# Weights of the RWKV turns split during the first feed-forward layer and kept in HBM; three float32r matmuls a tile in the pairs; separate signals in the triangular inverse

## The reference

```python
for l in range(2):
    x = x + 0.5 * rmsnorm(swiglu(rmsnorm(x, g1), wg, wu, wd), g2)          # d_ff 2816
    proj = rmsnorm(x, gm) @ w_in[l]                                        # columns A | B | C | G
    oa = rwkv7(A)      # 8 heads x 64, matrix state, token shift, vector decay
    ob = rglru(B)      # conv of width 4, gates, scan
    oc = hgrn2(C)      # 4 heads x 128
    m = (sig(G0)*(oa@proj_a) + sig(G1)*(ob@proj_b) + sig(G2)*(oc@proj_c)) @ w_out
    x = x + rmsnorm(m, gp)
    x = x + 0.5 * rmsnorm(swiglu(rmsnorm(x, g3), wg2, wu2, wd2), g4)
```

## Time and profile before

| | |
|---|---|
| median of 3 runs | 2145.59 us (2145.29 to 2145.84) |
| the profiled execution | 2146.02 us, span on the core 2143.9 us |
| TensorE busy, its clock | 2092.4 us (98%), 1.00 (2.4 GHz) |
| DVE, ACT, POOL busy | 1322.6, 817.9, 39.3 us |
| DMA | 252.13 MB, 118 GB/s over the span |

### The profile page before, as it was taken

How to read it: one execution, slowest core, us unless ns; L and a number is a source line. 1 busy time by engine, 2 the same in 40 slices (tenths; PEclk the granted TensorE clock), 3 DMA queues, 4 the chain that set the end, 5 groups by cost and what they waited for, 6 DMA issues and landing times.

```text
span 2143.9 us, 30994 instructions
## 1 busy us (share of the span) xinstructions
PE 2092.4 (98%) x12624; PEld 1844.9 (86%) x12624; DVE 1322.6 (62%) x1987; ACT 817.9 (38%) x932; POOL 39.3 (2%) x74
## 2 busy tenths in 40 slices
PE   7999999999999999999999999999999999999998
PEld 6999997777766699999999999977777667999998
DVE  4564586776556676555376645766765576765644
ACT  5554451112143145554355534412121422455542
POOL 1000000000000000000000000000000000000000
PEclk9999999999999999999999999999999999999999
DMA  5434431111133243444434443211111323434442
GB/s 210 152 143 157 156 118 38 58 51 70 45 110 120 91 158 118 157 148 147 170 138 146 155 157 138 105 40 52 68 51 65 121 90 130 163 113 149 145 156 103
DMA packets 38067, 252.13 MB, mean 118 GB/s; under 512 B 4720, under 2 KB 4912, under 8 KB 9424
## 3 DMA queue, kind: packets, MB, share of 16 engines
q1 hardware_dynamic: 33120, 234.60, 30.7%
q0 software_dynamic: 4848, 16.13, 2.0%
HBM read 242.05 MB, written 8.67 MB: 117 GB/s over the span
## 4 chain that ended last, share of the span: by engine, by line
PE 85%; DVE 8%; ACT 3%; DVEq 2%; issue 1%; DMA 0%; SPq 0%; ACTq 0%
PE dps L600 42%; PE dps L539 15%; PE dps L489 11%; DVE tmp L1252 2%; PE mx L698 2%; PE mx L692 2%; PE mx L700 2%; ACT tmp L922 1%; PE mx L556 1%; PE mx L809 1%; DVEq L1717 1%; PE mx L845 1%; DVE tmp L1468 1%; DVE rs L1310 1%; DVE tmp L1598 1%
## 5 line engine op out<-in xcount | busy, mean ns | idle before, releaser
L539 PE MATMUL dps<-u,raw 128*128 128x320 f32 x1536 | 478.3, 439 | 0.0
L600 PE MATMUL dps<-uh,whi 128*128 128x320 f32 x1408 | 430.0, 305 | 16.2 <-DVE wlo L1249 15.8
L1249 DVE TENSOR_TENSOR wlo<-raw,whi 128x2048 fp32r<-128x2048 f32 x136 | 311.7, 2292 | 214.7 <-ACT whi L922 209.6
L600 PE MATMUL dps<-uh,wlo 128*128 128x320 f32 x1408 | 434.3, 308 | 0.0
L600 PE MATMUL dps<-ul,whi 128*128 128x320 f32 x1408 | 432.9, 307 | 0.0
L922 ACT ACTIVATE whi<-raw 128x2048 fp32r<-128x2048 f32 x138 | 262.9, 1905 | 380.2 <-PE dps L600 370.0
L539 PEld LDWEIGHTS dps<-u,raw 128*128 128x128 f32 x1536 | 269.5, 190 | 89.2 <-issue 13.7
L600 PEld LDWEIGHTS dps<-uh,whi 128*128 128x128 f32 x1408 | 264.8, 188 | 20.9 <-issue 16.9
L600 PEld LDWEIGHTS dps<-uh,wlo 128*128 128x128 f32 x1408 | 264.9, 188 | 0.0
L600 PEld LDWEIGHTS dps<-ul,whi 128*128 128x128 f32 x1408 | 263.9, 187 | 0.6
L600 PE MATMUL dps<-hfh,whi 128*128 128x320 f32 x704 | 220.4, 313 | 0.0
(11 more groups left out here) (302 smaller groups left out, 3022.1 us busy)
## 6 DMA issues: line engine op xcount, KB each, us to landing
raw<-in_wstream SPq DMA_DIRECT2D x220, 1024.0 KB, 4.8
hs<-in_st_hgrn POOLq DMA_DIRECT2D x8, 512.0 KB, 6.2
out_o_hgrn<-hs POOLq DMA_DIRECT2D x8, 512.0 KB, 2.9
sw<-in_smallw POOLq DMA_DIRECT2D x2, 1024.0 KB, 6.8
ss<-in_st_rwkv POOLq DMA_DIRECT2D x8, 256.0 KB, 3.9
out_o_rwkv<-ss POOLq DMA_DIRECT2D x8, 256.0 KB, 2.3
x<-in_xT SPq DMA_DIRECT2D x4, 320.0 KB, 4.5
out_yT<-x SPq DMA_DIRECT2D x4, 320.0 KB, 2.2
```

The source lines that it names most:

```text
L539: m = pe.matmul(dps[:, 2 * s + c, 0:T], w[:, k, c * P:(c + 1) * P], u[:, k, :], start=k == 0, stop=k == KD - 1, skip_group_check=True)
L600: m = pe.matmul(dps[:, 2 * half + c, 0:T], w[:, k, c * P:(c + 1) * P], v[:, k0 + k, :], start=first and k == 0 and i == 0, stop=last and k ...
L1249: return nc.vector.tensor_tensor(out, a, b, op)
```

## The change

- **Presplit.** In each turn of the first feed-forward loop and once behind it, POOL loads one of the 12 weight blocks of the RWKV turns (two halves of 512 KB, into the memory of `u`), ACT makes its float32r high half (into `wha`), DVE its low half in place (`presplit_hi`, `presplit_lo`), and POOL stores both to a new HBM tensor `split_store` (four stores of 512 KB), then loads the next block. The other kinds of block are loaded as before.
- **Turns.** In the pairs SP loads 24 blocks a layer of `split_store` instead of 12 of weights, each with the high and low part of half a block (`parts0`, `parts1`, in the memory of `raw`). A tile is three float32r matmuls (`turn_pieces`). The normed input is split too: high part `nh` in the memory of x (ACT, `high_normed`), low part `nl` in `wha` and `ovr` (DVE, `low_normed`). x is therefore stored to HBM before the pairs and fetched behind them. The first gate block waits for its buffer until the parts of the last turn are used.
- **Inverse.** `pt_done` becomes `tinv_done` and `tinvt_done`, `t_ready` becomes `tinv_ready` and `tinvt_ready`; from level 2 on the product for `tinvt` lies in other banks of PSUM, so that the next level's first product can start before the subtraction that reads it. The step 0 of `prepare` stands behind the first `tinv`, and steps 4 and 5 both in level 5.
- **Places of the tiles.** 48 tiles a pair as before, 21 instead of 26 of them in the inverse; behind the recurrence the parts of 0, 2, 4, 2, 1, 0, 3, 2 tiles become 1, 3, 5, 2, 1, 2, 3, 2. In HGRN2 head 3 five tiles move to the end of the head. `keep_busy` is 11 instead of 15, and in `border` one scaling stands between two halves of the low input.

The diff shows in turn PE's tiles, SP's loads, POOL's presplit and PE's order in the inverse:

```diff
-        dense_part = pieces(l, B_B + 3 * p, Q_B + 3 * p)
+        dense_part = turn_pieces(l, p)
...
+    def turn_pieces(l, p):
+        done = [0]
+        def some(n):
+            for i in range(done[0], done[0] + n):
+                j, part, c, k = i // 16, i // 8 % 2, i // 4 % 2, i // 8 % 2 * 4 + i % 4
+                b, g = B_B + 3 * p + j, 6 * p + i // 8
+                if i % 16 == 0:
+                    pair_wait(l, (Q_B + 3 * p + j) // 2, b % 2)
+                if i % 8 == 0:
+                    pe.wait_ge(turn_loaded[g % 2], (l * (NTURN // 2) + g // 2) * 16 + 16)
+                    if g < 2:
+                        pe.wait_ge(S["nl_ready"], l * 3 + 2 * g + 1)
+                hi, low = (parts[g % 2][:, a:a + 1024].rearrange("p (k n) -> p k n", k=4) for a in (0, 1024))
+                for t, (w, v) in enumerate(((hi, nh[:, k, :]), (hi, nl[k]), (low, nh[:, k, :]))):
+                    m = pe.matmul(dps[:, 2 * (b % 2) + c, 0:T], w[:, k % 4, c * P:(c + 1) * P], v,
+                                  start=k == 0 and t == 0, stop=k == KD - 1 and t == 2, skip_group_check=True)
+                if i % 8 == 7:
+                    m.then_inc(S["turn_done"], 1)
...
                 order = mixer_order()
-                for j in range(B_A, B_G0):
+                for j in range(B_A, B_B):
                     s = j % 2
                     raw_free(l, j)
                     load(l, 0, order[j - B_A] - s, s)
+                    if j == B_A + 3:
+                        sp.wait_ge(S["x_new"], l * 12 + 8)
+                        sp.dma_start(yT, x[:, :, :]).then_inc(S["x_spilled"], 16)
+                sp.wait_ge(S["presplit"], l * NTURN + NTURN)
+                for g in range(NTURN):
+                    if g < 2:
+                        raw_free(l, B_B + g)
+                    else:
+                        wait_turn(sp, l, g - 2)
+                    sp.dma_start(parts[g % 2][:, :].bitcast(F32), split_store[l * NTURN + g, :, :])\
+                        .then_inc(turn_loaded[g % 2], 16)
                 for j in range(B_G0, B_F2 + 2):
-                    raw_free(l, j)
+                    if j < B_G0 + 2:
+                        wait_turn(sp, l, NTURN - 2 + j - B_G0)
+                    else:
+                        raw_free(l, j)
                     load(l, 0, j - j % 2, j % 2)
+                    if j == B_G0 + 1:
+                        sp.wait_ge(S["x_spilled"], l * 16 + 16)
+                        sp.dma_start(x[:, :, :], yT).then_inc(S["x_back"], 16)
...
+                order = mixer_order()[B_B - B_A:]
+                for q in range(len(order) + 1):
+                    for h in range(2):
+                        g = l * NTURN + 2 * (q - 1) + h
+                        if q:
+                            pool.wait_ge(pre_lo[h], l * len(order) + q)
+                            pool.dma_start(split_store[g, :, 0:1024], pre_high[h].bitcast(F32)).then_inc(pre_stored[h], 16)
+                            pool.dma_start(split_store[g, :, 1024:2048], pre_low[h].bitcast(F32)).then_inc(pre_stored[h], 16)
+                    for h in range(2):
+                        if q:
+                            pool.wait_ge(pre_stored[h], (l * len(order) + q) * 32)
+                            pool.sem_inc(S["presplit"], 1)
+                        if q < len(order):
+                            pool.dma_start(pre_raw[h], wstream[l * NBLK + order[q], :, 1024 * h:1024 * h + 1024])\
+                                .then_inc(pre_loaded[h], 16)
...
-                dense_part(6)
+                dense_part(4)
                 for li in range(1, 6):
                     if li > 1:
-                        dense_part((4, 3, 3, 3)[li - 2])
-                    pe.wait_ge(S["ao_ready"], n * 6 + (li + 1))
-                    pe.wait_ge(S["t_ready"], n * 6 + li)
+                        dense_part(1)
                     if li == 4 and more:
                         key_sums(l, p + 1)
+                    pe.wait_ge(S["ao_ready"], n * 6 + (li + 1))
+                    pe.wait_ge(S["tinv_ready"], n * 5 + li)
+                    if li == 2:
+                        pe.wait_ge(S["tinvt_ready"], n * 5 + 1)
...
-                    dense_part(1)
+                    if li == 5 and more:
+                        rk_sum(l, p + 1)
+                    dense_part(2)
                     pe.wait_ge(S["z_ready"], n * 5 + li)
+                    if li > 1:
+                        pe.wait_ge(S["tinvt_ready"], n * 5 + li - 1)
                     for c in range(nt):
-                        pe.matmul(mx23[:, c * P:(c + 1) * P], tinvt[:, c, :], zs[:, c, :], start=True, stop=True)
+                        m = pe.matmul(mx23[:, c * P:(c + 1) * P], tinvt[:, c, :], zs[:, c, :], start=True, stop=True)
+                    if nt:
+                        m.then_inc(S["tinv_done"], 1)
                     for c in range(nch):
-                        m = pe.matmul(mx01[:, c * P:(c + 1) * P], zs[:, c, :], tinvt[:, c, :], start=True, stop=True)
-                    m.then_inc(S["pt_done"], 1)
-                dense_part(2)
+                        m = pe.matmul(product_at(li, c), zs[:, c, :], tinvt[:, c, :], start=True, stop=True)
+                    m.then_inc(S["tinvt_done"], 1)
+                dense_part(3)
```

More of the change, by code:

```diff
@@ L178, in trunk @@
         rs = sb("rs", T)
-        raw = [sb(f"raw{i}", BLK) for i in range(2)]
+        raw, parts = zip(*[shared(f"raw{i}", BLK, views=[(f"parts{i}", (BLK,))]) for i in range(2)])
         sw, whb = shared("sw", 4, 512, views=[("whb", (BLK,))])
@@ L276, in trunk @@
             rooms[f"P{i}"] = wpc[:, 1024 * i:1024 * i + 1024]
+        uflat = u[:, :, :].rearrange("p a t -> p (a t)")
+        pre_raw, pre_low, pre_high = ([v[:, 1024 * h:1024 * h + 1024] for h in range(2)] for v in (uflat, ulo, wha))
+        nl = [wha[:, T * k:T * k + T] for k in range(6)] + [ovr[:, 0, :], ovr[:, 4, :]]
         def full_half(h):
@@ L312, in trunk @@
         w_loaded = [sem("w_loaded0"), sem("w_loaded1")]
+        pre_loaded, pre_hi, pre_lo, pre_stored, turn_loaded = (
+            [sem(f"{n}{h}") for h in range(2)]
+            for n in ("pre_loaded", "pre_hi", "pre_lo", "pre_stored", "turn_loaded"))
         pair_free = [sem("pair_free0"), sem("pair_free1")]
@@ L476, in block_in @@
             def block_in(l, half, s):
-                pe.wait_ge(w_loaded[s], (l * (NBLK // 2) + half) * 16 + 16)
+                pe.wait_ge(w_loaded[s], landed(l, half))
             def pair_wait(l, qhalf, s):
@@ L986, in read_pair, with presplit_hi @@
                 return fn(dst, dps[:, 2 * s:2 * s + n, 0:T], f)
+            def presplit_hi(l, i):
+                for h in range(2):
+                    act.wait_ge(pre_loaded[h], l * (NTURN * 8) + 16 + i * 16)
+                    fn(pre_high[h], pre_raw[h], ACT.Copy).then_inc(pre_hi[h], 1)
             def ffn(l, b, f):
@@ L1003, in ffn @@
                         split_hi(l, 0, KF + j + 2, j % 2, f)
+                    if f == 0 and j == 1:
+                        presplit_hi(l, KF // 2)
                 if f == 0:
@@ L1172, in _, with high_normed @@
                 read_low_rank(0)
+                def high_normed(i):
+                    act.wait_ge((S["u_half"], S["u_full"])[i], l + 1)
+                    act.wait_ge(S["x_spilled"], l * 16 + 16)
+                    fn(nh[:, 4 * i:4 * i + 4, :], u[:, 4 * i:4 * i + 4, :], ACT.Copy).then_inc(S["nh_ready"], 1)
+                high_normed(0)
                 for h in (10, 11):
@@ L1180, in _ @@
                 high(l, 13)
+                high_normed(1)
                 read_low_rank(2)
@@ L1370, in split_lo, with presplit_lo @@
                 tt(wlo[s][:, :], raw[s][:, :], whi[s][:, :].bitcast(F32), ALU.subtract).then_inc(S["lo_ready"], 1)
+            def presplit_lo(l, i):
+                for h in range(2):
+                    dve.wait_ge(pre_hi[h], l * (NTURN // 2) + 1 + i)
+                    tt(pre_low[h], pre_raw[h], pre_high[h].bitcast(F32), ALU.subtract).then_inc(pre_lo[h], 1)
             def ffn(l, b, f):
@@ L1397, in ffn @@
                     split_lo(l, f, 0, KF + j, j % 2)
+                    if f == 0 and j == 3:
+                        presplit_lo(l, KF // 2)
                     if j in (4, 7, 10):
@@ L1804, in _, with low_normed @@
                 read_a(1)
-                normed(0)
+                normed(0).then_inc(S["u_half"], 1)
                 low_half(l, 8)
                 low_half(l, 9)
+                def low_normed(a, b):
+                    dve.wait_ge(S["nh_ready"], l * 2 + 1 + a // 4)
+                    for k in range(a, b):
+                        m = tt(nl[k], u[:, k, :], nh[:, k, :].bitcast(F32), ALU.subtract)
+                    m.then_inc(S["nl_ready"], 1)
+                low_normed(0, 4)
                 read_a(2)
@@ L1829, in _ @@
                 m.then_inc(S["e_ready"], 1)
+                low_normed(4, 6)
                 read_a(5)
@@ L1832, in _ @@
```

(2 more changed lines are left out.)

117 lines of the change are left out of this document (81 added, 36 removed).

## The result

| | before | changed |
|---|---|---|
| median of four runs | 2145.45 us | 2189.57 us |
| all runs | 2145.29 to 2145.84 | 2186.21 to 2200.73 |
| profiled execution, its span | 2146.0, 2143.9 | 2186.2, 2184.4 |
| mean granted clock | 1.00 | 0.986 |

The changed kernel is slower: the ratio is 1.0214, with a 95% interval of 1.0178 to 1.0251. The forecast was 2124.5 us with a range up to 2150. The sign was wrong, and the time lies outside the range.

What follows compares the result with a forecast made beforehand. PE was taken to bound feed-forward layers and pairs, with a DVE chain close behind in the pairs. -30 + 5.5 + 5.8 - 2.2 = -21 us on 2146.0 gave 2125, median 2124.5 us; range 2112 to 2136, wider 2100 to 2150.

Steps and rivals of the forecast that it cites:

- The presplit loop: First feed-forward layer: load, split, store and next load take 14.1 us against 13.8 a turn, +5.5 us over 22 turns.
- A turn over 15 us: Sign in the first feed-forward layer that the forecast is wrong and the presplit's loop sets the pace.
- The loop's upper bound: Presplit loop in the first feed-forward layer: at most 15.7 us a turn, a loss of 42 us in all.
- The loop of the presplit sets the pace: Rival, first feed-forward layer: 5.24 MB at 340 GB/s makes a turn 15.4 us, total 2154; chance 0.22.
- First turn late: Start of the first feed-forward layer: PE waits for block 3, 2.9 us a layer, +5.8 us in all.
- Arithmetic hidden: First feed-forward loop: the presplit's Copies and subtractions on ACT and DVE are covered, with 0.7 us to spare.
- Pairs, 15.0 us a layer: RWKV pairs: cheaper float32r tiles gain 2.8, 4.1, 4.1 and 4.0 us in pairs 0 to 3, -30 us in two layers.
- Gate block: Pair 3: PE waits 2.7 us for the gate block's load, cutting that pair's gain from 6.7 to 4.0 us.
- HGRN2's end: End of HGRN2 head 3: five tiles cover the idle 1.06 us ahead of the projections, -2.2 us.
- Borders: Borders: four fewer fills of 0.44 us change nothing, as PE waits for DVE; bounds 0 and -1.0 at each of five.
- Parts come late: Rival, pairs: SP's doubled loads lose 1 us on every second part, 24 us, total 2148; chance 0.08.
- PE keeps the whole gain: Rival, pairs and presplit: DVE chains give way and the presplit is hidden, total 2105; chance 0.13.

Runs made afterwards that it cites:

- Raw doubled: The change with raw blocks going alternately to two pairs of half buffers, each load issued a turn ahead, same bytes: 2138.1 us, ratio 0.9949.
- the best kernel: On top of late start, pair 3's two gate tiles moved to its end and HGRN2 head 3's five tiles back in front: 2113.4 us, ratio 0.9849.
- the 64 KB transfers: The changed kernel's own loop with every DMA cut to an eighth of its bytes, except each layer's first block: 2137.9 us.
- the second run: The change with all presplit Copies and subtractions, but only the first block of a layer loaded and stored: 2138.2 us.
- the pairs alone: The change without its presplit loop, one block split a layer and its parts standing in for all 24: 2124.1 us, ratio 0.9901.
- late start: Raw doubled, with no presplit in the loop's first turn and two blocks split in the down part: 2134.4 us.

## Why the prediction was wrong

Between the 2125 us forecast for the profiled execution and the 2186 measured lie 61 us. The presplit has 57 of them (68.2 lost; 11.3 forecast, 5.5 for the loop and 5.8 for the first turn), the end of HGRN2 has 4.

- **The presplit loop, "middle 14.1: 0.25 us a turn, +5.5 us": this step failed.** The mechanism was seen: a loop that must close in a turn. One term of its sum was mis-sized. Arithmetic 2.3 and stores with their hand-overs 6.0 us came within what was taken (2.3 and 4.5 to 6.2). The load was taken as 5.8 to 7.2 us, from a load of the kernel before beside one stream load. The load that the chain waits for took 8.9, beside a stream load, the end of the other half's load and its stores. So the loop took 17.3 instead of 14.1 us. The turn follows the loop from 13.8 us on, so the 32.2 us of layer 0 are 3.4 of the first turn and 2.9 for each of the ten after it, up to 3.3 in the mean of the later ones. A turn over 15 us was the prediction's own sign of this rival, and it is there.
- **The range left out its own bound.** The loop's upper bound, 15.7 us a turn and 42 us in all, gives 2124.5 - 5.5 + 42 = 2161, but the range "from the bounds of the loop and the gate" ends at 2136 and the wider one at 2150. The result lies above 2161 too.
- **The clock had no term.** The trace of before shows none: 1.00 throughout the stretches read. Inside the loop it seems to cost nothing of its own: the chain there holds no TensorE, and half clock takes the place of waiting (22.7 + 10.2 us, against 32.2 us lost in layer 0). That is argued from the trace; no run has the loop without half clock. Outside it costs in full: behind the gate block's wait, and in the pairs.
- **The rival was the right mechanism with the wrong price.** "The loop of the presplit sets the pace", chance 0.22, gave 2154 from bytes over 340 GB/s. Its break-even, 1.2 us a turn, is summed rightly; but its price came from bandwidth, and the loop was bound by its chain. Raw doubled shows both: same bytes, 13.9 us a turn. The Trainium skill's limit of some 358 GB/s a core ("DMA: Bandwidth & Descriptors", Specifications), by which the turn would be 14.6 us by estimate, does not bind this core, which runs alone: 368 GB/s with raw doubled and 376 in the best kernel, both over 50 us. The Trainium skill's price of one DMA, 2.0 us and its bytes at 436 GB/s (same page, Anatomy of one DMA), fits the 64 KB transfers (2.15 us by estimate; 2.2 measured for the loads, 2.4 and 2.6 for the stores). For the whole load it gives an estimated 3.2 us, and the one that the chain waits for took 8.9.
- **First turn late, 2.9 us a layer:** 3.4 us in layer 0 (43.45 to 47.01 between two starts, less 0.14), with a stretch of 6.8 us at half clock that begins in the gap; 5.3 in layer 1, with 3.4 us behind it.
- **Arithmetic hidden:** right, by the second run, where loads come in time.
- **Pairs, 15.0 us a layer:** measured 15.2 and 14.1, in part by luck, since the errors of the parts cancel. Pairs 1 and 2 gained 5.1 each (4.7 in pair 1 of layer 1; forecast 4.1), pair 0 4.1 and 4.2 (2.8), pair 3 with what follows it 0.9 and 0.2 (4.0). What was forecast for pairs 1 and 2 is there: the wait at level 1 is 1.57 us where 2 were forecast, 7.56 us pass from variance product to key transposes, and the tiles start 0.145 us apart:

```profile
418.40 0.31 PE L623 MATMUL dps<-nh,parts 128*128 128x320 f32 x1
418.54 0.31 PE L623 MATMUL dps<-ovr,parts 128*128 128x320 f32 x1
418.69 0.31 PE L623 MATMUL dps<-nh,parts 128*128 128x320 f32 x1
...
436.95 1.24 PE L784 MATMUL mx<-ho 128*128 128x128 f32 x9 [1.57 <-DVE ho L1372]
```

- **Gate block, 2.7 us:** 2.9, as in the list of waits; the load of its block lands 5.2 us after its issue at 597.8. What was missed is again the clock (PE busy, clock, DMA share, GB/s), right behind the wait that ended at 603.1:

```profile
603.00:606.00 3.00, 2.87 (x7) 0.50 0.07 25
607.00:610.00 3.00, 3.00 (x20) 1.00 0.00 0
```

- **HGRN2's end, -2.2 us:** +1.6. The five tiles do fill the idle time ahead of the projections, but cost more behind HGRN2 (1.9 us in layer 0) than they free in it (1.3), and a stretch of half clock falls into head 3 in both layers. With them back in place the stretch is gone.
- **Borders 0:** 56.6 and 56.5 us. Right.
- **Parts come late:** no wait on `parts` in the profile of the change or of the pairs alone. **PE keeps the whole gain:** no; its sum gives 2106, not 2105.
- **A reading:** the three lines that the prediction names hold 42 + 15 + 11 = 68% of the chain, two thirds and not three fifths. Nothing in the sum hangs on it.

What stays open: what exactly brings the 17.1 us at half clock in the pairs, which begin 2.3 to 2.6 us behind the end of the wait for the recurrence in pairs 0, 1 or 2 when they come at all; and why the feed-forward part with the presplit is 3.4, 3.6, 7.5 and 9.6 us above before in the four profiles with late start, where DMA is at a share of 1.00.

## What to carry to other kernels

A loop of load, arithmetic, store and next load through one buffer has a period of its own, and its DMA terms must be taken from the traffic that the loop itself makes, not from the trace without it; where its middle estimate is within a few us of the turn, double the buffer first. Here the same bytes cost about 3 us a turn as a chain and 0.1 with the load a turn ahead. A median over all DMAs of a group can hide the one that the chain waits for (6.3 against 8.9 us). And where TensorE is near its bound, a wait can cost more than its length: look at the granted clock behind it, and try to move the wait, which took 5.1 us off pair 3 here. Idle products in the waits showed no gain.

## What was not expected of the hardware

- In the changed kernel's first feed-forward layers each gap of 3.0 us or more came with 3.4 or 6.8 us at half clock (13 matmuls in 3 us, against 20 to 23), which began between 2.1 us ahead of the gap's end and 0.8 us behind it; those of 0.5 to 1.9 us did not. Between these there is no clear line: in the best kernel a gap of 2.0 us was followed by 3.4 us at half clock and one of 2.2 was not. Where TensorE is the bound, such a stretch costs half its length (the 17.1 us ones 7.4, a little less).
- In the pairs, where TensorE is busy 58.9 of 62.0 us and each wait is under 2 us, stretches of 17.1 us at half clock came in some executions and not in others, always at the same place in a pair; each cost 7.4 us. They go some way to explain why the changed kernel's runs spread over 15 us and those of before over 0.6: the longest execution of the change, 2200.7 us, had a mean clock of 0.982 where the shortest had 0.986. By estimate that is 18 us more at half clock, one stretch more, and about 8 of the 14.5 us.
- The core moved 368 and 376 GB/s of loads and stores together over 50 us, at a share of 1.00.
